# HGRN's diagonal level as a product of query and keys, summed by a square of ones in two fp32r passes, and products with the weights' low part last

## The chip, the core and the metric

The kernel runs on one core of one Trainium2 chip. The core has five engines that run side by side, each through its own list of instructions in order, and wait for each other on semaphores: TensorE (PE in the profile; its weight loads are listed apart as PEld), VectorE (DVE), ScalarE (ACT), GpSimd (POOL) and SyncE (SP), which issues the DMA transfers. Matrix products go into PSUM banks; everything else lies in SBUF. The metric is the device time of one execution in microseconds. Each version is run several times and the median is taken.

## The reference

Two transformer blocks on 256 tokens of width 1024, all in float32. The first has three parts side by side behind one large projection: HGRN2 (a gated linear recurrence in both directions), a spatial gating unit and two gates; then a feed-forward layer and a gated embedding. The second is a Fourier mixer, a feed-forward layer, a retention mixer and a feed-forward layer. What the change touches most is HGRN2's part inside a chunk, for each of 8 heads and each direction:

```python
b = jnp.cumsum(gc, axis=2)                       # gc: log of the forget gates
diff = b[:, :, :, None, :] - b[:, :, None, :, :]
decay = jnp.exp(jnp.minimum(diff, 0.0)) * mask[:, :, None]
scores = jnp.einsum('bhtk,bhsk,bhtsk->bhts', qc, kc, decay)
o_intra = jnp.einsum('bhts,bhsv->bhtv', scores, vc)
```

On the diagonal (t = s) the decay is one, so the score there is the plain sum over k of the query times the key, and for both directions together it is the query times the sum of the two keys. All other products are `x @ w` with float32 weights.

## The kernel before

**Numbers in two parts.** TensorE multiplies fp32r, a rounded form of float32, in one pass. So each operand is kept as a high and a low part (`w_hi`, `w_lo`; `ht`, `gt` and others have `_hi` and `_lo` too), and a product is three matmuls: low x by high w, high x by high w, high x by low w. The weights come as one stream of chunks of 1 MB through three raw buffers. For chunk w, ACT makes `w_hi` (`split_hi`, L1006), then DVE makes `w_lo` as raw less `w_hi` (`split_lo`, L1438), which also frees the raw buffer for the next transfer (SP, L398). Four chunks have a place in `w_hi` and `w_lo`. `tick(w)` on both engines makes the parts of chunk w + 4; on DVE a tick may also hold an `ada` step (L1447), a weight chunk of a small product done there. `wait_chunk` on TensorE waits for `w_lo`, and with it for `w_hi`.

**Order.** The order is written out by hand on each engine: what stands first runs first. TensorE's functions are `wide_chunk` (24 matmuls of 512 columns: two token tiles, four rows of weights, three parts), `feat` (the same turned, 48 matmuls of 256 columns), `outer` (a chunk for tile 0 or tile 1, 12 matmuls of 512 columns) and the small pieces between them. A result of 1024 columns lies in one of two PSUM pairs, which ACT or DVE has to evacuate before it is used again; small results lie in four banks `tp`, each claimed for a numbered job.

**HGRN in levels.** The heads are done in two halves of four. For a half, `head_gates` makes from three projections the query `qf`, `qb`, the keys `kf`, `kb` and the gates `tf`, `tb`. `levels` then builds the scores in eight levels: level 0 is the diagonal, level lv > 0 holds the pairs whose positions part in blocks of 2^(lv-1). On each level TensorE does a chunk of another projection (`zi`, `zg` in half 0, `ga`, `gb` in half 1) and then 8 float32 products of 128 x 128 of `sk` and `sq`, which the profile lists as 16 records (L697). ACT fills `sq` and `sk` for a level by four copies (`stage_level`, L1091 to L1094; one copy, L1084, for the queries of level 0) once TensorE has read the level before and DVE has updated queries and keys. DVE reads the scores into `at` through a mask (`take_scores`, L1659) and multiplies totals, queries and keys by the gates for the next level (L1648, L1628, L1638). In half 0, level 0, DVE also multiplies the gating unit's `u` (`gate_u`, L1769). ACT evacuates a pair on every odd level (L1015); in half 0, level 5, the function changes to Silu, for which ACT loads a table.

**The other places.** Behind HGRN `outer` multiplies by `wb` and `wa`; the tiles of `a_out` are turned on TensorE and split into `gt` in two halves for each token tile (L1024 on ACT, L1514 on DVE), and `wait_split("ta", 2)` waits for both. In the retention mixer's gate (`rg`, chunks 0 to 7) DVE multiplies head by head (`gated_head`, L2018), and TensorE turns the products from chunk 5 on; then `outer` multiplies by `ro`. `gate_rows` (L638) adds up a diagonal with a square of ones in two fp32r passes: two matmuls of 512 columns for each bank.

## Time and profile before

| | before |
|---|---|
| median of 3 runs | 1138.7 us (1138.3 to 1139.54) |
| profiled execution | 1139.04 us, span 1136.6 us |
| mean granted TensorE clock | 0.998 |
| TensorE busy | 1127.7 us, 99% |
| DVE busy | 852.0 us, 75% |
| ACT busy | 545.2 us, 48% |
| chain that ended last, TensorE's share | 94% |

The span runs from the first to the last instruction; the execution holds 2.4 us around it. Records of TensorE overlap, since their ends are modelled: how fast it goes is seen from start to start. A name like `w_lo<-raw,w_hi` says what is written and read.

### The profile page before, as it was taken

The numbers are of one execution on the slowest core, as the hardware profiler recorded it, in microseconds if no ns is written. First come the engines' busy times: TensorE is split into PE (matmuls) and PEld (weight loads), VectorE is DVE, ScalarE is ACT, GpSimd is POOL, SyncE is SP. The second block draws the span as 40 slices with busy tenths as digits, with TensorE's granted clock in tenths as the row PEclk, the third lists the DMA queues.
The fourth block names the chain that finished last, engine by engine and source line by source line (L and its number), as shares of the span: only waits on it lengthen the run. The fifth ranks groups of instructions, "written<-read, shape, count | busy, mean of one in ns | idle before, by whom it ended". The sixth has DMA issues, their size and how long they took to land.

```text
span 1136.6 us, 14091 instructions
## 1 busy us (share of the span) xinstructions
PE 1127.7 (99%) x5852; PEld 964.3 (85%) x5852; DVE 852.0 (75%) x958; ACT 545.2 (48%) x552; POOL 31.4 (3%) x51
## 2 busy tenths in 40 slices
PE   9999999999999999999999999999999999999997
PEld 8998998888888888889888888889988888888886
DVE  7899879977766768566677677479967866867685
ACT  6756456634744444355645353453332435444441
POOL 1000000000100000000000000000001000000000
PEclk9999999999999999999999999999999999999999
DMA  8864554448567777544477778558753754886760
GB/s 290 306 231 153 179 201 148 149 177 310 189 229 289 267 286 286 218 155 149 148 262 260 299 255 314 204 212 297 285 212 111 255 226 168 307 301 253 298 228 37
DMA packets 37966, 259.81 MB, mean 229 GB/s; under 512 B 4240, under 2 KB 4752, under 8 KB 7440
## 3 DMA queue, kind: packets, MB, share of 16 engines
q1 hardware_dynamic: 36000, 251.67, 60.1%
q0 software_dynamic: 1616, 7.08, 1.7%
q8 instruction: 46, 0.75, 0.3%
q10 hardware_dynamic: 288, 0.17, 0.1%
q14 instruction: 16, 0.13, 0.0%
HBM read 257.86 MB, written 1.05 MB: 228 GB/s over the span
## 4 chain that ended last, share of the span: by engine, by line
PE 94%; DVE 2%; DMA 2%; ACT 1%; issue 1%; POOLq 0%; POOL 0%; DVEq 0%; ACTq 0%
PE pair L477 47%; PE pair L542 20%; PE pair L503 10%; PE pair L558 4%; PE tp L606 3%; PE tp L697 3%; DMA raw<-stream 1%; PE tp L978 1%; ACT w_hi L1006 1%; PE pair L916 1%; PE tp L724 1%; DVE w_lo L1438 1%; PE tp L954 1%; PE tp L903 1%; PE pair L824 1%
## 5 line engine op out<-in xcount | busy, mean ns | idle before, releaser
L1438 DVE TENSOR_TENSOR w_lo<-raw,w_hi 128x2048 fp32r<-128x2048 f32 x180 | 409.0, 2288 | 77.5 <-ACT w_hi L1006 77.1
L1006 ACT ACTIVATE w_hi<-raw 128x2048 fp32r<-128x2048 f32 x180 | 344.3, 1917 | 228.4 <-DMA raw<-stream 140.6
L477 PE MATMUL pair<-w_hi,ht_lo 128*128 128x512 f32 x784 | 310.1, 396 | 0.0
L477 PE MATMUL pair<-w_lo,ht_hi 128*128 128x512 f32 x784 | 305.6, 390 | 0.0
L477 PE MATMUL pair<-w_hi,ht_hi 128*128 128x512 f32 x784 | 305.3, 389 | 0.0
L477 PEld LDWEIGHTS pair<-w_lo,ht_hi 128*128 128x128 f32 x784 | 147.1, 188 | 31.2
L477 PEld LDWEIGHTS pair<-w_hi,ht_lo 128*128 128x128 f32 x784 | 147.3, 188 | 29.4 <-DVE ht_lo L1498 0.5
L477 PEld LDWEIGHTS pair<-w_hi,ht_hi 128*128 128x128 f32 x784 | 147.4, 188 | 29.0
L1447 DVE SCALAR_TENSOR_TENSOR raw<-raw,crow 128x1024 f32<-128x1024 f32 x112 | 132.3, 1219 | 0.7 <-DMA raw<-stream 0.7
L542 PE MATMUL pair<-w_hi,gt_lo 128*128 128x512 f32 x272 | 107.1, 394 | 0.5 <-DVE w_lo L1438 0.3
L542 PE MATMUL pair<-w_lo,gt_hi 128*128 128x512 f32 x272 | 106.0, 390 | 0.0
L542 PE MATMUL pair<-w_hi,gt_hi 128*128 128x512 f32 x272 | 105.9, 389 | 0.0
L1124 ACT ACTIVATE prod<-pair 128x512 f32<-128x512 f32 x33 | 19.8, 599 | 153.6 <-PE pair L477 153.6
L1576 DVE TENSOR_TENSOR prod<-prod,pair 128x512 f32<-128x512 f32 x33 | 22.7, 688 | 93.9 <-ACT prod L1124 93.9
L503 PE MATMUL pair<-ht_hi,w_lo 128*128 128x256 f32 x304 | 86.4, 284 | 0.0
L503 PE MATMUL pair<-ht_lo,w_hi 128*128 128x256 f32 x304 | 86.0, 283 | 0.0
L503 PE MATMUL pair<-ht_hi,w_hi 128*128 128x256 f32 x304 | 86.0, 283 | 0.0
L542 PEld LDWEIGHTS pair<-w_hi,gt_lo 128*128 128x128 f32 x272 | 51.1, 188 | 11.7 <-DVE w_lo L1438 0.7
L542 PEld LDWEIGHTS pair<-w_lo,gt_hi 128*128 128x128 f32 x272 | 51.1, 188 | 10.7
L542 PEld LDWEIGHTS pair<-w_hi,gt_hi 128*128 128x128 f32 x272 | 51.1, 188 | 10.2
L503 PEld LDWEIGHTS pair<-ht_hi,w_hi 128*128 128x128 f32 x304 | 58.4, 192 | 0.0
L503 PEld LDWEIGHTS pair<-ht_hi,w_lo 128*128 128x128 f32 x304 | 58.3, 192 | 0.0
(289 smaller groups left out, 1370.2 us busy)
## 6 DMA issues: line engine op xcount, KB each, us to landing
raw<-stream SPq DMA_DIRECT2D x236, 1024.0 KB, 4.9
raw<-stream SPq DMA_DIRECT2D x8, 256.0 KB, 6.2
xres<-x SPq DMA_DIRECT2D x2, 512.0 KB, 5.0
prow<-rows POOLq DMA_DIRECT2D x1, 1024.0 KB, 10.6
xres<-x POOLq DMA_DIRECT2D x2, 512.0 KB, 4.9
dt<-decay POOLq DMA_DIRECT2D x1, 1024.0 KB, 10.8
csr<-dft POOLq DMA_DIRECT2D x1, 768.0 KB, 6.0
sgw<-sg_wT POOLq DMA_DIRECT2D x1, 512.0 KB, 5.8
```

What stands on the lines that cost most here:

```text
L477: mm = pe.matmul(pair[use % 2][:, t, :], a[:, 4 * c + k, t * P:(t + 1) * P], b[:, w % WS, k * 512:(k + 1) * 512], start=(c == 0 and k == 0 ...
L503: mm = pe.matmul(pair[use % 2][:, c, m * S:(m + 1) * S], a[:, k, m * P:(m + 1) * P], b[:, k, :], start=(k == 0 and n == 0), stop=(k == KT ...
L542: mm = pe.matmul(pair[(use + t) % 2][:, half, :], src(a, k0 + 2 * c + k, t), wsp[b][:, (w + c) % WS, k * D + half * 512:k * D + half * 512 ...
L558: mm = pe.matmul(dst, src(a, 2 * c + k, t), wsp[b][:, (w + c) % WS, k * D + a0:k * D + b0], start=(c == first and k == 0 and m == 0), stop ...
L606: mm = pe.transpose(tp[k % BANKS][:, n * P:(n + 1) * P], a, idn[:, 0:P])
L697: mm = pe.matmul(tp[k % BANKS][:, hd * P:(hd + 1) * P], sk[:, hd, s * P:(s + 1) * P], sq[:, hd, s * P:(s + 1) * P], start=True, stop=True)
L724: mm = pe.matmul(tp[k % BANKS][:, hd * P:(hd + 1) * P], at[:, s, hd, t * P:(t + 1) * P], vv[:, s, (HH * half + hd) * P:(HH * half + hd + 1 ...
L1006: sc.activation(w_hi[:, w % WS, :], raw[:, n % RAW, :], ACT.Copy).then_inc(hi_done, 1)
L1124: sc.activation(prod[:, j % 2, :, :], pair[(use + j) % 2][:, :, 0:256], ACT.Silu).then_inc(silu_done, 1)
L1438: v.tensor_tensor(w_lo[:, w % WS, :], raw[:, n % RAW, :], whi32[:, w % WS, :], ALU.subtract).then_inc(raw_done, 1)
L1447: ins = v.scalar_tensor_tensor(out=src, in0=src, scalar=1.0, in1=crow[:], op0=ALU.mult, op1=ALU.mult, accum_out=mod[:, 2 * a + half:2 * a ...
L1576: v.tensor_tensor(prod[:, j % 2, :, :], prod[:, j % 2, :, :], pair[(use + j) % 2][:, :, 256:512], ALU.mult).then_inc(evac[(use + j) % 2], 1)
```

## The change

**Diagonal level.** DVE now multiplies `sk = kf + kb` by `qf`, ACT rounds the product to `qk_hi`, DVE takes the rest as `qk_lo`, and TensorE sums both over the partitions with a square of ones: every row of the result holds the sums, and the mask takes the diagonal. This stands on TensorE behind the chunk of level 1 and right ahead of level 1's scores. The copy of `qf` to `sq` is gone; the copy to `qk_hi` stands on ACT behind the evacuation of the third projection and ahead of a `w_hi` split. DVE reads level 0's scores together with level 1's. `gate_u` moves from level 0 to level 4, and ACT waits for it (`b_out`) on level 5.

**Low part last.** For the first token tile of a chunk (`wide_first`, the first half of `feat`, `outer` at t = 0), TensorE waits for `w_hi` alone, does all products with it, then waits for `w_lo` and does those with `w_lo`. The numbers of matmuls stay.

**Two orders.** `wa` starts with one half of the split and waits for the other at chunk 2. `gated_head(0)` stands ahead of the tick of `rg` chunk 4 instead of behind its loop.

```diff
+            def wide_first(w, use, c):
+
+                pe.wait_ge(hi_done, pieces_done(w))
+                for n, (a, b) in enumerate(passes(ht, wsp)):
+                    if n == 2:
+                        wait_chunk(w)
+                    for k in range(4):
+                        pe.matmul(pair[use % 2][:, 0, :], a[:, 4 * c + k, 0:P], b[:, w % WS, k * 512:(k + 1) * 512],
+                                  start=(c == 0 and n == 0 and k == 0), stop=(c == 1 and n == 2 and k == 3))
...
             def wide_chunk(w, use, c):
-                wait_chunk(w)
                 if c == 0:
                     claim_pair(use)
-                for t in range(TT):
-                    wide_part(w, use, c, t)
+                wide_first(w, use, c)
+                wide_part(w, use, c, 1)
...
+                    if t == 0 and (c, t) not in middle:
+                        pe.wait_ge(hi_done, pieces_done(w + c))
+                        for n, (a, b) in enumerate([(1, 0), (0, 0), (0, 1)]):
+                            if n == 2:
+                                wait_chunk(w + c)
...
+                def own():
+                    pe.wait_ge(hg_qk, half + 1)
+                    for s in range(2):
+                        claim(job + s)
+                        for n in range(2):
+                            mm = pe.matmul(tp[(job + s) % BANKS][:], ones_r[:], qk[n][:, :, s * P:(s + 1) * P],
+                                           start=(n == 0), stop=(n == 1))
+                        mm.then_inc(tp_done, 1)
+
                 for lv in range(8):
                     wide_chunk(W0[name] + lv, USE[name] + lv // 2, lv % 2)
+                    if lv == 0:
+                        continue
+                    if lv == 1:
+                        own()
                     pe.wait_ge(hg_staged, 8 * half + lv + 1)
-                    if lv == 0:
-                        pe.wait_ge(hg_sk0, half + 1)
...
-                  before={(0, 0): lambda: wait_split("ta", 2), (0, 1): lambda: wait_split("ta", 4)},
+                  before={(0, 0): lambda: wait_split("ta", 1), (2, 0): lambda: wait_split("ta", 2),
+                          (0, 1): lambda: wait_split("ta", 4)},
...
                 if lv == 0:
-                    if half:
-                        act.wait_ge(tp_done, JOB["pa"] + 16)
-                    act.wait_ge(evac[USE["qa" if half == 0 else "qb"] % 2], USE["qa" if half == 0 else "qb"] // 2 + 1)
-                    sc.activation(sq[:], qf[:], ACT.Copy).then_inc(hg_staged, 1)
+                    act.wait_ge(hg_sk0, half + 1)
+                    sc.activation(qk[0][:], sk[:], ACT.Copy).then_inc(hg_staged, 1)
                     return
...
+                        if half == 0 and lv == 5:
+                            act.wait_ge(b_out, 2)
                         evacuate(dst, use, func)
...
-                v.tensor_tensor(sk[:], kf[:], kb[:], ALU.add).then_inc(hg_sk0, 1)
+                link(v.tensor_tensor(sk[:], kf[:], kb[:], ALU.add))
+                v.tensor_tensor(sk[:], sk[:], qf[:], ALU.mult).then_inc(hg_sk0, 1)
                 gates(1, tb)
                 dve.wait_ge(hg_staged, 8 * half + 1)
+                v.tensor_tensor(qk[1][:], sk[:], as_f32(qk[0][:]), ALU.subtract).then_inc(hg_qk, 1)
                 link(v.tensor_tensor(qb[:], qf[:], tb[:], ALU.mult))
                 v.tensor_tensor(qf[:], qf[:], tf[:], ALU.mult).then_inc(hg_qupd, 1)
...
                 for lv in range(8):
-                    take_scores(half, lv)
+                    if lv == 1:
+                        take_scores(half, 0)
+                    if lv:
+                        take_scores(half, lv)
...
-                    if half == 0 and lv == 0:
+                    if half == 0 and lv == 4:
                         gate_u()
                     tick(W0[name] + lv)
...
             for c in range(5):
+                if c == RH:
+                    gated_head(0)
                 tick(W0["rg"] + c)
...
-            gated_head(0)
             gated_head(1)
```

How this moves the instructions, at three places. First DVE in half 0, from the keys to the first updates, before (a bracket names the semaphores waited for: `step` is DVE's own last result, `hg_staged` ACT's copies):

```order
L1612 TENSOR_TENSOR sk<-kf,kb 128x1024 [waits step]
L1598 TENSOR_SCALAR tb<-tb,lbt 128x256 x4
L1601 TENSOR_SCALAR tb<-tb 128x1024 [waits step]
L1615 TENSOR_TENSOR qb<-qf,tb 128x1024 [waits hg_staged,step]
L1616 TENSOR_TENSOR qf<-qf,tf 128x1024 [waits step]
L1438 TENSOR_TENSOR w_lo<-raw,w_hi 128x2048 [waits hi_done]
L1659 COPY_PREDICATED at<-msk,tp 128x4x128 [waits tp_done] x2
L1628 TENSOR_TENSOR qf<-qf,tf 128x512 [waits hg_staged,hg_qupd]
```

and now, where lines of the kernel have shifted:

```order
L1663 TENSOR_TENSOR sk<-kf,kb 128x1024 [waits step]
L1664 TENSOR_TENSOR sk<-sk,qf 128x1024 [waits step]
L1649 TENSOR_SCALAR tb<-tb,lbt 128x256 x4
L1652 TENSOR_SCALAR tb<-tb 128x1024 [waits step]
L1667 TENSOR_TENSOR qk_lo<-sk,qk_hi 128x1024 [waits hg_staged,step]
L1668 TENSOR_TENSOR qb<-qf,tb 128x1024
L1669 TENSOR_TENSOR qf<-qf,tf 128x1024 [waits step]
L1489 TENSOR_TENSOR w_lo<-raw,w_hi 128x2048 [waits hi_done]
L1681 TENSOR_TENSOR qf<-qf,tf 128x512 [waits hg_staged,hg_qupd]
```

A product and a subtraction have come in ahead of qb and qf, and the reading of level 0's scores has gone from here.

ACT in half 0 around level 5, before:

```order
L1094 ACTIVATE sk<-kb 128x32x16
L1015 ACT_TABLE_LOAD
L1015 ACTIVATE zg<-pair 128x2x512 [waits w_used]
L1006 ACTIVATE w_hi<-raw 128x2048 [waits w_used,landed0]
L1091 ACTIVATE sq<-qf 128x16x32 [waits tp_done,hg_kupd,hg_qupd]
```

and now:

```order
L1143 ACTIVATE sk<-kb 128x32x16
L1061 ACT_TABLE_LOAD [waits b_out]
L1061 ACTIVATE zg<-pair 128x2x512 [waits w_used]
L1052 ACTIVATE w_hi<-raw 128x2048 [waits w_used,landed0]
L1140 ACTIVATE sq<-qf 128x16x32 [waits tp_done,hg_kupd,hg_qupd]
```

The wait for `gate_u` stands ahead of the table load; both stand ahead of level 6's copies.

TensorE in half 0 between the chunk of level 1 and that of level 2, before:

```order
L477 MATMUL pair<-w_lo,ht_hi 128x512
L697 MATMUL tp<-sq,sk 128x128 [waits sgu_read,hg_staged]
L697 MATMUL tp<-sq,sk 128x128 x3
L697 MATMUL tp<-sq,sk 128x128 [waits sgu_read]
L697 MATMUL tp<-sq,sk 128x128 x3
L477 MATMUL pair<-w_hi,ht_lo 128x512 [waits evac0,raw_done]
```

and now:

```order
L727 MATMUL tp<-qk_hi,ones 128x512 [waits lo_done,hg_qk]
L727 MATMUL tp<-qk_lo,ones 128x512
L727 MATMUL tp<-qk_hi,ones 128x512 [waits rows_read]
L727 MATMUL tp<-qk_lo,ones 128x512
L742 MATMUL tp<-sq,sk 128x128 [waits sgu_read,hg_staged]
L742 MATMUL tp<-sq,sk 128x128 x3
L742 MATMUL tp<-sq,sk 128x128 [waits sgu_read]
L742 MATMUL tp<-sq,sk 128x128 x3
L482 MATMUL pair<-w_hi,ht_lo 128x512 [waits hi_done,evac0]
```

The sums of level 0 have come in ahead of level 1's scores; behind the chunk of level 0 nothing stands any more, and the chunk of level 2 begins with a wait for w_hi.

## Rows read from the trace of the kernel before

**Rows 1.** The page's first part, whole span: busy time, share, instructions of each engine.
```profile
PE 1127.7 (99%) x5852; PEld 964.3 (85%) x5852; DVE 852.0 (75%) x958; ACT 545.2 (48%) x552; POOL 31.4 (3%) x51
```

**Rows 2.** The chain that ended last; columns: start us, length us, what.
```profile
83.56 1.78 PE tp L697 x16
...
836.66 0.92 PE tp L638 x4
```

**Rows 3.** Timeline of TensorE; columns: start, length, instruction, in brackets idle time before.
```profile
83.40 0.27 PE L697 MATMUL tp<-sq,sk 128*128 128x128 f32 x1
...
119.60 0.27 PE L697 MATMUL tp<-sq,sk 128*128 128x128 f32 x1
...
182.11 0.27 PE L697 MATMUL tp<-sq,sk 128*128 128x128 f32 x1
...
244.94 0.50 PE L542 MATMUL pair<-w_hi,gt_lo 128*128 128x512 f32 x1 [0.25 <-DVE gt_lo L1514]
...
881.27 0.33 PE L606 MATMUL tp<-idn,gg 128*128 128x128 f32 x1 [0.16 <-DVE gg L2018]
...
925.52 0.39 PE L542 MATMUL pair<-w_lo,gt_hi 128*128 128x512 f32 x1
926.20 0.50 PE L542 MATMUL pair<-w_hi,gt_lo 128*128 128x512 f32 x1 [0.29 <-DVE w_lo L1438]
```

**Rows 4.** Timeline of VectorE (DVE), around the levels and the three waits.
```profile
77.33 1.23 DVE L1615 TENSOR_TENSOR qb<-qf,tb 128x1024 f32<-128x1024 f32 x1
78.59 1.23 DVE L1616 TENSOR_TENSOR qf<-qf,tf 128x1024 f32<-128x1024 f32 x1
79.73 2.29 DVE L1438 TENSOR_TENSOR w_lo<-raw,w_hi 128x2048 fp32r<-128x2048 f32 x1
81.94 1.34 DVE L1659 COPY_PREDICATED at<-msk,tp 128x512 f32<-128x512 uint8 x2
83.17 0.68 DVE L1628 TENSOR_TENSOR qf<-qf,tf 128x512 f32<-128x512 f32 x1
...
85.57 1.28 DVE L1769 TENSOR_TENSOR u<-u,vg 128x512 f32<-128x512 f32 x2
86.77 2.28 DVE L1438 TENSOR_TENSOR w_lo<-raw,w_hi 128x2048 fp32r<-128x2048 f32 x1
...
114.29 2.28 DVE L1438 TENSOR_TENSOR w_lo<-raw,w_hi 128x2048 fp32r<-128x2048 f32 x1
...
136.59 2.29 DVE L1438 TENSOR_TENSOR w_lo<-raw,w_hi 128x2048 fp32r<-128x2048 f32 x1 [3.97 <-ACT w_hi L1006]
...
234.79 1.22 DVE L1812 TENSOR_TENSOR gb<-gb,pair 128x1024 f32<-128x1024 f32 x1 [1.60 <-PE pair L542]
...
243.59 1.29 DVE L1514 TENSOR_TENSOR gt_lo<-tp,gt_hi 128x512 fp32r<-128x512 f32 x2 [2.09 <-ACT gt_hi L1024]
...
877.72 2.29 DVE L1438 TENSOR_TENSOR w_lo<-raw,w_hi 128x2048 fp32r<-128x2048 f32 x1 [1.52 <-ACT w_hi L1006]
```

**Rows 5.** Timeline of ScalarE (ACT), in the levels.
```profile
72.72 1.92 ACT L1006 ACTIVATE w_hi<-raw 128x2048 fp32r<-128x2048 f32 x1
...
81.57 0.66 ACT L1094 ACTIVATE sk<-kb 128x512 f32<-128x512 f32 x1
...
110.25 1.28 ACT L1015 ACT_TABLE_LOAD   x1
112.56 1.03 ACT L1015 ACTIVATE zg<-pair 128x1024 f32<-128x1024 f32 x1 [1.03 <-PE pair L477]
...
116.85 0.62 ACT L1094 ACTIVATE sk<-kb 128x512 f32<-128x512 f32 x1
...
180.25 0.66 ACT L1094 ACTIVATE sk<-kb 128x512 f32<-128x512 f32 x1
```

**Rows 6.** Busy time by stretch: us, PE, PEld, DVE, ACT, POOL, clock (PEclk), DMA, GB/s.
```profile
1130.20:1132.30 2.10, 0.00 (x0) 0.00 (x0) 1.44 (x4) 0.51 (x2) 0.35 (x1) 1.00 0.00 0
1132.40:1136.60 4.20, 0.00 (x0) 0.00 (x0) 1.54 (x3) 0.00 (x0) 0.10 (x1) 0.50 0.34 125
```

More of the change, by code:

```diff
@@ L499, in feat @@
                 wv = [a[:, w % WS, :].rearrange("p (k n) -> p k n", k=KT) for a in wsp]
-                for m in range(2):
+                for n, (a, b) in enumerate([(wv[0], ht[1]), (wv[0], ht[0]), (wv[1], ht[0])]):
+                    if n == 2:
+                        wait_chunk(w)
                     for k in range(KT):
-                        for n, (a, b) in enumerate(passes(wv, ht)):
-                            mm = pe.matmul(pair[use % 2][:, c, m * S:(m + 1) * S], a[:, k, m * P:(m + 1) * P],
-                                           b[:, k, :], start=(k == 0 and n == 0), stop=(k == KT - 1 and n == 2))
+                        pe.matmul(pair[use % 2][:, c, 0:S], a[:, k, 0:P], b[:, k, :], start=(k == 0 and n == 0),
+                                  stop=(k == KT - 1 and n == 2))
+                for k in range(KT):
+                    for n, (a, b) in enumerate(passes(wv, ht)):
+                        mm = pe.matmul(pair[use % 2][:, c, S:2 * S], a[:, k, P:2 * P], b[:, k, :],
+                                       start=(k == 0 and n == 0), stop=(k == KT - 1 and n == 2))
                 mm.then_inc(w_used, 1)
@@ L528, in outer, with whole_part @@
                 m = max(0, n - 4)
+                last = n - 1
                 order = [(c, t) for c in range(m) for t in range(TT)] + [(c, t) for t in range(TT) for c in range(m, n)]
-                for c, t in order:
-                    if (c, t) in before:
-                        before[c, t]()
-                    if t == 0:
-                        wait_chunk(w + c)
-                    if c == 0:
-                        claim_pair(use + t)
+                def whole_part(c, t):
                     for half in range(2):
```

38 lines of the change are left out of this document (31 added, 7 removed).

## The prediction

> **What bounds the kernel now.** I read the share of busy time first [rows 1]: TensorE (PE) is busy 99% of the span, VectorE (DVE) 75%, ScalarE (ACT) 48%. So a microsecond of matmuls saved is a microsecond of kernel, if nothing else comes late in its place. Next the chain that ended last [rows 2]: in the eight levels of one half of HGRN it is TensorE alone, a chunk of 24 matmuls of 512 columns and then 16 records of 128 columns, 1.78 us. Then the timeline of TensorE [rows 3]: a matmul's record is 0.39 long (925.52), though the next one starts 0.23 after it where nothing waits (4 in 0.92 [rows 2]). The bracketed idle time counts from the record's end, so a wait costs 0.16 more than it says, and the first record behind it is longer too (0.50). Behind the start-up only three waits for another engine are long enough to be listed: at 244.94, at 881.27 and at 926.20. Last, the timelines of DVE and ACT in the levels [rows 4, 5]: DVE stands there without a gap, and ACT's copies into sq and sk, which the scores of a level wait for, end little ahead of TensorE.
>
> **What TensorE is spared.** The diagonal level was 16 records, 1.78 us. It is now 4 matmuls of 512 columns, for which the nearest row is the gate's rows, also a square of ones against fp32r: 4 in 0.92 [rows 2]. Saved: 0.86 us a half, 1.72 in all, if the rest of the level keeps up. The reordered products are as many as before, of the same shapes, so I take them at nothing. A wait whose semaphore is already up costs nothing that shows: the scores at 83.40 [rows 3] stand behind two and have no idle time ahead.
>
> **The three waits that go.** At 244.94 TensorE waits for the second half of a split (gt_lo); it now needs the first of DVE's two operations alone, which take 1.29 together from 243.59 [rows 4] and so ended 0.6 us earlier: saved 0.25 + 0.16 + 0.11 (longer record) = 0.52. At 881.27 it waits for gg; the product now stands ahead of the split at 877.72 instead of behind it, in the 1.52 us in which DVE waited for ACT there [rows 4]; two of gg's four operations, about 1.25 us, fit in: 0.16 + 0.16 + 0.05 = 0.37. At 926.20 it waits for w_lo, ready at 926.15; the low part is now wanted 8 matmuls (1.8 us) later than the first: 0.29 + 0.16 + 0.11 = 0.56. Together 1.45 us. Everywhere else low-part-last removes a wait that wasn't there.
>
> **What is added: the first level in half 0.** Before, sq was a copy made long ahead, and the level's sk needed one addition. Now DVE has to make (kf+kb)*qf and its low part, both ahead of qb and qf. An operation of this size takes 1.26 where the next waits for it (77.33 to 78.59) and 1.14 where not (78.59 to 79.73) [rows 4]. The addition of sk turns from the second kind into the first, the product adds 1.14, the subtraction 1.14: 0.12 + 1.14 + 1.14 = 2.40 us. ACT's copy to qk_hi (about 1.0) runs under DVE's gates and hides. But qf ends 2.40 later, and level 1's copies start on it: the last ended at 81.57 + 0.66 = 82.23 [rows 5], and will end at 84.63. TensorE wanted them at 83.40 [rows 3] and will want them 0.86 earlier, at 82.54. It starts at 84.68 instead of 83.40, plus 0.05 for the cold start: **1.33 us later than before**, a stall of 2.2 where 0.86 was to be won.
>
> **The second place in half 0: gate_u.** DVE is saturated, so its delay lasts. Its updates for level 1 wait for the copies (84.63, seen at 84.72) instead of starting at 83.17, and end 2.40 later at 87.12. A split (2.21, from 79.73 to 81.94) and the displaced reading of the diagonal's scores (1.23, 81.94 to 83.17) bring it to 90.56 where it was at 86.77 + 2.21 = 88.98: 1.58 late (gate_u's 1.20 at 85.57 has gone from there). It keeps that to the end of level 5's key updates, 114.29 + 1.58 = 115.87. There gate_u now stands, to 117.15. ACT, which evacuated a pair at 112.56, has a new wait for gate_u (b_out) ahead of that. The built order shows the wait ahead of the **table load** too, which before ran in the open at 110.25 and now takes its 1.28 behind the wait: evacuation at 118.46. Behind it on ACT are a split and the copies of level 6: from 112.56 to 116.85 + 0.62 that was 4.91 us [rows 5], so they end at 123.37. TensorE, 1.33 late, would ask at 119.60 + 1.33 = 120.93 and starts at 123.42: 3.82 + 0.05 = **3.87 us later than before** (this holds the 1.33). What is late next is DVE: it is then about as late as TensorE, plus 1 to 2 us; its idle 3.97 us ahead of 136.59 [rows 4] takes that up, and no TensorE step waits on it before.
>
> **Half 1.** The same head without gate_u: copies ended at 180.25 + 0.66 = 180.91, now 183.31; TensorE starts at 183.36 instead of 182.11: **1.25 + 0.05 = 1.30 us later**. DVE's wait for the copies and the displaced reading make it 1.55 + 1.23 = 2.8 us late against TensorE's 1.30. In both halves the copies of the other levels lie further ahead of TensorE than level 1's 1.17 us, and I reckon that they bear the 1.5 between the two. DVE's 1.60 idle at 234.79 takes the rest up, so the wait at 244.94 isn't reached by it.
>
> **Moves that I cost at nothing.** The w_hi split that now stands behind the qk_hi copy comes 5 us later (72.72 [rows 5] to 77.6). Its w_lo is made when DVE gets there, now at 82.13, and TensorE wants the chunk two chunks behind level 1's scores: that is the cover, some 7 us. The stream's transfers follow DVE's splits, so they shift by the same 1.5 to 2.4 us; a chunk is loaded four chunks ahead. No DMA, no Pool instruction and nothing on SP is moved.
>
> **Sum.** Against the profiled execution (1139.04 us, span 1136.6): + 3.87 + 1.30 - 1.45 = **+3.7 us**, 1142.8. The runs shown have their median at 1138.7, 0.3 below it, so I forecast **1142.4**. Its own range is 1141.3 to 1143.4: the extra behind a stall is 0 to 0.11 at three places, the diagonal's four matmuls change nothing while a stall follows them, and DVE's additions may be 10% off over 2.4 and 1.6.
>
> **Rivals.** (a) The added DVE work is hidden: then 1138.7 - 1.72 - 1.45 = **1135.5**. It decides at the slack of level 1's copies, 83.40 - 82.23 = 1.17 less the 0.86 that TensorE comes earlier: 0.3 us, against 2.40 added. Against it: three DVE operations would have to be 0.1 us long, and rows of just this size are 1.1 to 1.2. For it: only that the copies might begin without qf, which the order of ACT denies. Chance 0.09.
> (b) Only the stalls at level 1 come; gate_u is early enough, or the table load hides. Then half 0 keeps 1.33: 1138.7 + 1.33 + 1.30 - 1.45 = **1139.9**. It needs DVE to make up over 2 us between 90 and 116, where its timeline has no gap. Chance 0.08.
> (c) The clock falls in a stall. TensorE did nothing from 1130.2 to 1132.3 and was granted 1.00 of 2.4 GHz; from 1132.4 on it was granted 0.50, 1.2 GHz [rows 6]. The stalls forecast here are 2.2, 2.5 and 2.2 us long, about where that fall stands. While the clock is down the same matmuls take about twice as long; a fall for some 4 us costs 2. One in the first stall would be swallowed by the second; one in the second or third gives **1144.4**, both 1146.4. Against it: matmuls stand thick on either side, and at the end none followed. Chance 0.18. The Trainium skill ("TensorE: Matmul & The Clock Gate", section "HAM oscillation — how this bites in real kernels") has it that idle gaps between bursts of matmuls put the clock back to its low level, and that every return is paid for. By that rule the time would be (c)'s; the trace agrees that idleness brings the fall, and has no gap inside the kernel that would show how it treats one of 2 us.
> (d) A copy of a later level is late too, or a saving is not had (DVE is over 1 us later than TensorE in half 1, or when the head outputs are due): up to 1.5 more, **1143.9**. Chance 0.10.
> (e) Low-part-last doesn't shorten anything, since the waits at 244.94 and 926.20 only move inside the chunk: 1143.5, in (d)'s price. The rows speak against it: w_lo is up 1.4 us before it is wanted.
>
> **Chances.** Forecast 0.55, (a) 0.09, (b) 0.08, (c) 0.18, (d) with (e) 0.10. Two in ten are left out by 1139.0 to 1145.0: (a) below, half of (c) above. A change of 0.2% (2.3 us, about what a measurement of this kernel can tell from none) parts 1136.4 and 1141.0: faster 0.09, (b) and a little of the forecast's own spread within it 0.15, slower 0.76.
>
> **What would show it.** In the profile after: TensorE idle some 2 us ahead of level 1's scores in both halves and 2.3 to 2.5 ahead of level 6's in half 0, put down to ACT's copies into sk; DVE's qf ending near 82.2; the table load near 117 instead of 110; no listed waits for gt_lo, gg and w_lo; the four ones matmuls in 0.92. Wrong it would be if TensorE reached level 1's scores later than its copies, if the table load stood at 110 or if 0.50 stood in the clock's row in the middle of the span.

## The result, and the profile of the changed kernel

The changed kernel takes **1143.4 us** in the median of 6 runs (1142.0 to 1145.4), the kernel before 1137.9 in 6 runs beside them: a ratio of 1.0047, 95% interval 1.0037 to 1.0057. It is slower by 5.5 us, half a per cent. Forecast were 1142.4, and 1139.0 to 1145.0. In a second set of runs it was 1142.8 (5 runs) against 1137.6, again 1.0047.

The profiled execution took 1141.98 us, span 1139.5. The page's first part, which answers [rows 1], shows that TensorE did less and that the kernel is longer all the same:

```profile
PE 1126.6 (99%) x5828; PEld 961.7 (84%) x5828; DVE 856.4 (75%) x962; ACT 544.6 (48%) x552; POOL 31.4 (3%) x51
```

The waits of TensorE (what waited, for whom: us in all, times, the longest). The three of before at 244.94, 881.27 and 926.20 [rows 3] are gone, and three new ones stand there, all for ScalarE's last copy into sk:

```profile
PE tp L742 <- ACT sk L1143: 4.6, 3, 1.9
PE tp L778 <- POOL expo L411: 1.0, 1, 1.0
PE tp L640 <- DMA idn<-ident: 0.7, 1, 0.7
```

The timeline of TensorE at these three places: the first and the last sum of ones (L727), then level 1's scores (L742); the last matmul ahead of level 6's scores and these; level 1 again in half 1. It answers [rows 3]:

```profile
80.64 0.39 PE L727 MATMUL tp<-qk_hi,ones 128*128 128x512 f32 x1
...
81.34 0.39 PE L727 MATMUL tp<-qk_lo,ones 128*128 128x512 f32 x1
83.67 3.61 PE L742 MATMUL tp<-sq,sk 128*128 128x128 f32 x16 [1.94 <-ACT sk L1143]
...
121.38 0.39 PE L489 MATMUL pair<-w_lo,ht_hi 128*128 128x512 f32 x1
122.51 2.05 PE L742 MATMUL tp<-sq,sk 128*128 128x128 f32 x16 [0.74 <-ACT sk L1143]
...
184.05 0.39 PE L727 MATMUL tp<-qk_lo,ones 128*128 128x512 f32 x1
186.37 2.05 PE L742 MATMUL tp<-sq,sk 128*128 128x128 f32 x16 [1.94 <-ACT sk L1143]
```

Two things are to be seen. The stalls stand where they were forecast, though the middle one is short. And the 16 records at 83.67 took 3.61 us where the same 16 take 2.05 at 186.37: the clock fell. The windows view (us, then busy time of PE, PEld, DVE, ACT, POOL, then the granted clock) of that stretch has it at half, 1.2 GHz, where the rest of the levels has 1.00:

```profile
83.80:87.10 3.30, 3.30 (x17) 3.30 (x18) 3.30 (x5) 2.52 (x2) 0.00 (x0) 0.51 0.78 263
```

VectorE's timeline, which answers [rows 4]. The product (L1664) and the subtraction (L1667) stand ahead of qf (L1669), and gate_u (L1822) now behind level 5's key updates:

```profile
74.34 1.22 DVE L1664 TENSOR_TENSOR sk<-sk,qf 128x1024 f32<-128x1024 f32 x1
...
77.62 1.23 DVE L1667 TENSOR_TENSOR qk_lo<-sk,qk_hi 128x1024 fp32r<-128x1024 f32 x1
...
80.01 1.23 DVE L1669 TENSOR_TENSOR qf<-qf,tf 128x1024 f32<-128x1024 f32 x1
...
114.90 1.28 DVE L1822 TENSOR_TENSOR u<-u,vg 128x512 f32<-128x512 f32 x2
```

ScalarE's timeline, which answers [rows 5]. The table load ran at 110.25 before, right behind the copies; it now waits 4.88 us for gate_u and has the evacuation, a split and level 6's copies behind it:

```profile
70.85 1.02 ACT L1266 ACTIVATE kb<-pair 128x1024 f32<-128x1024 f32 x1
...
82.96 0.66 ACT L1143 ACTIVATE sk<-kb 128x512 f32<-128x512 f32 x1
...
110.77 0.62 ACT L1143 ACTIVATE sk<-kb 128x512 f32<-128x512 f32 x1
116.27 1.28 ACT L1061 ACT_TABLE_LOAD   x1 [4.88 <-DVE u L1822]
117.56 1.03 ACT L1061 ACTIVATE zg<-pair 128x1024 f32<-128x1024 f32 x1
...
121.84 0.62 ACT L1143 ACTIVATE sk<-kb 128x512 f32<-128x512 f32 x1
```

**Executions start differently.** This evacuation of kb, ahead of all that the diagonal's change touches, began at 70.85; in the execution on which the sum was made, ScalarE's timeline has it at 71.82:

```profile
71.82 1.02 ACT L1218 ACTIVATE kb<-pair 128x1024 f32<-128x1024 f32 x1
```

The kernel before was therefore profiled once more (`before_again`, below): there kb began at 70.84 and the execution took 1137.82. Against this twin with the same start the changed kernel's span is 1139.5 - 1135.5 = 4.0 us longer; against the first profile, put on the same start, 1139.5 - (1136.6 - 0.97) = 3.9. The sum was 3.7.

### The profile page after: what moved, and what is told of

Read it like the earlier page. It is cut to its first block, busy times and chain, and to the rows that moved or that the text cites. A ratio compares the mean times of both kernels' runs of the same rounds, so it can differ in the third digit from the quotient of the medians.

```text
span 1139.5 us, 14049 instructions
## 1 busy us (share of the span) xinstructions
PE 1126.6 (99%) x5828; PEld 961.7 (84%) x5828; DVE 856.4 (75%) x962; ACT 544.6 (48%) x552; POOL 31.4 (3%) x51
## 4 chain that ended last, share of the span: by engine, by line
PE 93%; DVE 3%; issue 2%; ACT 1%; DMA 0%; DVEq 0%; POOLq 0%; POOL 0%; ACTq 0%
PE pair L489 26%; PE pair L482 18%; PE pair L572 11%; PE pair L554 11%; PE pair L519 5%; PE pair L515 5%; PE pair L592 4%; PE tp L640 3%; PE tp L742 1%; PE tp L1024 1%; PE pair L962 1%; PE tp L769 1%; PE tp L1000 1%; PE tp L949 1%; PE pair L869 1%
## 5 line engine op out<-in xcount | busy, mean ns | idle before, releaser
L489 PE MATMUL pair<-w_hi,ht_lo 128*128 128x512 f32 x456 | 177.9, 390 | 0.0
L489 PE MATMUL pair<-w_lo,ht_hi 128*128 128x512 f32 x456 | 177.6, 389 | 0.0
L489 PE MATMUL pair<-w_hi,ht_hi 128*128 128x512 f32 x456 | 177.4, 389 | 0.0
L489 PEld LDWEIGHTS pair<-w_hi,ht_lo 128*128 128x128 f32 x456 | 85.6, 188 | 17.9 <-DVE ht_lo L1549 0.5
L482 PE MATMUL pair<-w_hi,ht_lo 128*128 128x512 f32 x328 | 92.6, 404 | 0.0
L482 PE MATMUL pair<-w_hi,ht_hi 128*128 128x512 f32 x328 | 88.0, 390 | 0.0
L482 PE MATMUL pair<-w_lo,ht_hi 128*128 128x512 f32 x328 | 87.8, 390 | 0.0
L482 PEld LDWEIGHTS pair<-w_hi,ht_lo 128*128 128x128 f32 x328 | 58.6, 189 | 9.8
L554 PE MATMUL pair<-w_hi,gt_lo 128*128 128x512 f32 x136 | 53.3, 392 | 0.0
L554 PE MATMUL pair<-w_lo,gt_hi 128*128 128x512 f32 x136 | 53.0, 390 | 0.0
L554 PE MATMUL pair<-w_hi,gt_hi 128*128 128x512 f32 x136 | 52.9, 389 | 0.0
L417 POOL TENSOR_TENSOR st<-st,expo 128x1 f32<-128x1 f32 (+1 forms) x32 | 23.7, 743 | 913.7 <-DVE st L1516 572.3
L519 PE MATMUL pair<-ht_hi,w_lo 128*128 128x256 f32 x152 | 43.0, 283 | 0.0
```

The lines of the kernel that those rows point to most:

```text
L417: g.tensor_tensor(st[:, r, 2, 0:w], st[:, r, 1, 0:w], expo[:, 0:w], ALU.pow).then_inc(rstd_done, 1)
L482: pe.matmul(pair[use % 2][:, 0, :], a[:, 4 * c + k, 0:P], b[:, w % WS, k * 512:(k + 1) * 512], start=(c == 0 and n == 0 and k == 0), stop= ...
L489: mm = pe.matmul(pair[use % 2][:, t, :], a[:, 4 * c + k, t * P:(t + 1) * P], b[:, w % WS, k * 512:(k + 1) * 512], start=(c == 0 and k == 0 ...
L519: mm = pe.matmul(pair[use % 2][:, c, S:2 * S], a[:, k, P:2 * P], b[:, k, :], start=(k == 0 and n == 0), stop=(k == KT - 1 and n == 2))
L554: mm = pe.matmul(pair[(use + t) % 2][:, half, :], src(a, k0 + 2 * c + k, t), wsp[b][:, (w + c) % WS, k * D + half * 512:k * D + half * 512 ...
```

## The experiments

Theory: nearly all of the loss is three stalls of TensorE ahead of level 1 (twice) and level 6, made by VectorE's two added operations ahead of qf and by gate_u with the table load; the rest is the clock that falls in stalls. Rivals: the reordered products cost time themselves; the sums of ones do; the spread has nothing to do with the clock.

### Half of the change at a time

`e1_no_diag` is the kernel before with only this kind of edit, in wide_chunk, feat and outer, with the wait for ta's split cut in two and gated_head(0) moved:

```diff
-                wait_chunk(w)
+                pe.wait_ge(hi_done, pieces_done(w))
...
+                for n, (a, b) in enumerate(passes(ht, wsp)):
+                    if n == 2:
+                        wait_chunk(w)
```

> The kernel before with only the reordered products (the weights' low part last, the split wait in wa cut in two, gated_head(0) moved up); the diagonal level stays as it was. The stall theory: the products do the same matmuls in another order and cost nothing, the three waits of before at 244.94 (0.52), 881.27 (0.37) and 926.20 (0.56) are gone, so 1137.9 - 1.45 = 1136.4 us, and no new wait on TensorE. The rival, that the new order itself costs time (other weights loaded one after the other, the low part's matmuls late), wants 1138.5 us or more here, since some of the +5.5 us must then lie in these products.

Measured: 1136.9 us (11 runs), ratio 0.9995, interval 0.9986 to 1.0003. Waits of TensorE:

```profile
PE tp L765 <- POOL expo L409: 1.0, 1, 1.0
PE tp L638 <- DMA idn<-ident: 0.5, 1, 0.5
```

Nothing new, and none of the three left. By the medians the gain is 0.6 us, below what can be told from no change; by the traces it is 1.3 to 1.4: from the start of level 1's scores to the last matmul 1127.39 - 82.34 = 1045.05 us, against 1128.78 - 82.43 = 1046.35 in before_again and 1129.86 - 83.40 = 1046.46 in the first profile. The reordered products cost nothing; the first rival falls.

`e2_diag_only` is the kernel before with all the other edits:

```diff
+                link(v.tensor_tensor(sk[:], kf[:], kb[:], ALU.add))
+                v.tensor_tensor(sk[:], sk[:], qf[:], ALU.mult).then_inc(hg_sk0, 1)
...
+                v.tensor_tensor(qk[1][:], sk[:], as_f32(qk[0][:]), ALU.subtract).then_inc(hg_qk, 1)
...
-                    if half == 0 and lv == 0:
+                    if half == 0 and lv == 4:
                         gate_u()
```

> The kernel before with only the diagonal level changed (product, two passes of ones, gate_u at level 4, ScalarE's wait for b_out). The stall theory: the measured +5.5 us and the 1.45 us of the waits that are not won back here, 1137.9 + 5.5 + 1.4 = 1144.8 us, with three TensorE waits of about 1.9, 0.7 to 2.5 and 1.9 us ahead of the scores of levels 1, 6 and 1. Without any loss to the clock it would be 1137.9 + 5.2 = 1143.1 us. The rival (the reordered products cost) wants 1142.5 us or less.

Measured: 1144.0 us (5 runs), before 1137.5, ratio 1.0057 (1.0044 to 1.0070). Its waits have the three stalls and, besides, those for gt_lo and gg, as before:

```profile
PE tp L710 <- ACT sk L1110: 4.6, 3, 2.0
...
PE pair L544 <- DVE gt_lo L1532: 0.2, 1, 0.2
PE tp L608 <- DVE gg L2041: 0.2, 1, 0.2
```

That is 0.8 us less than expected, and more than 1142.5, where the rival would have it. The loss is the diagonal's, and the other half of the change gives back about a microsecond of it. The wait for w_lo that before had at 926.20 is not in this list, though the products stand here in their old order: w_lo was made by 929.20, and the matmul that needs it started at 931.34.

### gate_u back at its place

`e3_gate_early`, against the changed kernel:

```diff
-                    if half == 0 and lv == 4:
+                    if half == 0 and lv == 0:
                         gate_u()
...
-                        if half == 0 and lv == 5:
-                            act.wait_ge(b_out, 2)
```

> The changed kernel with gate_u back at level 0 and ScalarE's wait for b_out gone; everything else as changed. By the prediction's terms the stall ahead of level 6 goes and those of level 1 stay: 1137.9 - 3.2 + 1.33 + 1.30 + 2.5 of it that come back only if DVE's 2.56 us now delay another level; if none is delayed, 1139.9 us, plus what the clock takes in the first stall, about 1.7 us as in the profiled execution, which nothing swallows any more: 1141.6 us. If instead gate_u at level 0 falls due right behind the already late level 1, level 2 is late by up to 2.5 us and the time stays near 1143. ScalarE's wait of 4.9 us ahead of the table load should be gone and the sigmoid-to-Silu table load start at once behind the copies of level 5.

Measured: 1140.4 us (7 runs, 1139.3 to 1142.6), before 1137.5, ratio 1.0027 (1.0016 to 1.0038), where the changed kernel has 1.0047: 2.3 us less. The wait ahead of level 6 is gone: 3.9 us in two waits are left. The table load runs right behind level 5's copies:

```profile
111.51 0.62 ACT L1143 ACTIVATE sk<-kb 128x512 f32<-128x512 f32 x1
112.15 1.28 ACT L1061 ACT_TABLE_LOAD   x1
114.63 1.02 ACT L1061 ACTIVATE zg<-pair 128x1024 f32<-128x1024 f32 x1 [1.20 <-PE pair L489]
```

The profiled execution took 1142.59, though, and here the clock fell in both stalls, also behind the second (this row of the windows view is of half 1):

```profile
186.30:189.50 3.20, 3.20 (x15) 2.91 (x14) 3.20 (x4) 2.81 (x3) 0.00 (x0) 0.51 0.77 307
```

Of the 7 runs the two longest, 1142.6 and 1142.4, have a mean clock of 0.996 and the other five, 1139.3 to 1141.0, of 0.998 or 0.999. The four runs at 0.999 took 1139.3 to 1140.4, around the 1139.9 that was expected without a fall; the two longest lie above the 1141.6 expected with one fall, and the profiled one of them had two. The other branch, level 2 late, is not seen.

### The table load alone

`e5_table_early`, against the changed kernel (`tiny` is a new tile of four numbers that nothing reads):

```diff
                         if half == 0 and lv == 5:
+                            sc.activation(tiny[:], col[:, 0:4], ACT.Silu)
                             act.wait_ge(b_out, 2)
```

> The changed kernel with one Silu of four numbers put ahead of ScalarE's wait for b_out, so that the table load of 1.28 us stands ahead of that wait instead of behind it. The theory: level 6's copies end 1.28 us earlier. In executions in which TensorE was not held up before, the stall ahead of level 6 falls from 2.5 to 1.2 us; in those like the profiled one, with 0.9 us left of it, it goes. So 0.9 to 1.3 us less than the changed kernel of the same call. If instead VectorE's gate_u alone made level 6 late and the table load was beside it, the time stays that of the changed kernel.

Measured: 1141.2 us (5 runs) against 1142.8 for the changed kernel beside it: 1.6 less, where 0.9 to 1.3 was expected. ScalarE's and then TensorE's timeline:

```profile
112.99 1.28 ACT L1293 ACT_TABLE_LOAD   x1
116.15 0.21 ACT L1293 ACTIVATE tiny<-col 128x4 f32<-128x4 f32 x1 [1.87 <-PE pair L490]
117.80 1.03 ACT L1062 ACTIVATE zg<-pair 128x1024 f32<-128x1024 f32 x1 [1.44 <-DVE u L1824]
...
122.08 0.62 ACT L1144 ACTIVATE sk<-kb 128x512 f32<-128x512 f32 x1
```

```profile
123.19 1.95 PE L743 MATMUL tp<-sq,sk 128*128 128x128 f32 x16
```

The load is hidden and the 16 records at 123.19 have no idle time ahead; in this execution TensorE had lost time to a fall in the first stall, as in the changed kernel's. The wait for gate_u is still there, 1.44 us. The intervals of the two ratios overlap (1.0022 to 1.0047 here, 1.0034 to 1.0060 there), so the size rests on the trace: from the start of kb (72.43 here) to the end of level 6's copies it is 122.08 + 0.62 - 72.43 = 50.27 us, in the changed kernel 121.84 + 0.62 - 70.85 = 51.61, 1.34 more. The table load is a good half of the second stall, gate_u's place the rest.

### Clock and stalls apart

`e6_keep_warm`, against the changed kernel. The added matmuls write a PSUM bank that the scores then overwrite:

```diff
+                    warm_up = 9 if lv == 1 else 10 if lv == 6 and half == 0 else 0
+                    if warm_up:
+                        claim(job + 2 * lv)
+                    for _ in range(warm_up):
+                        pe.matmul(tp[(job + 2 * lv) % BANKS][:], ones_r[:], qk[0][:, :, 0:P], start=True, stop=True)
                     pe.wait_ge(hg_staged, 8 * half + lv + 1)
```

> The changed kernel with matmuls of 512 columns that nothing reads (0.23 us each) in TensorE's stalls: nine ahead of the wait for level 1's copies in each half, ten ahead of that for level 6's in the first. They fill the stalls and do not lengthen them by themselves. If the clock falls because TensorE stands still there, no record at half clock is left but the last one at the end, no execution is above 1142, and the median is before + 3.7 = 1141.2 to 1141.6 us on this chip, against 1143 for the changed kernel. If the falls have nothing to do with the stalls, falls and the spread to 1145 remain. If the whole +5.5 is stall and the clock has no part, the time stays 1143.

Measured: 1142.3 us (5 runs, 1142.1 to 1142.9), before 1137.6, ratio 1.0040 (1.0027 to 1.0053). TensorE in half 0 and half 1, and the same windows row as above:

```profile
82.01 2.26 PE L741 MATMUL tp<-qk_hi,ones 128*128 128x512 f32 x9
84.15 2.05 PE L747 MATMUL tp<-sq,sk 128*128 128x128 f32 x16
...
120.49 2.49 PE L741 MATMUL tp<-qk_hi,ones 128*128 128x512 f32 x10
122.95 2.05 PE L747 MATMUL tp<-sq,sk 128*128 128x128 f32 x16
...
184.71 2.26 PE L741 MATMUL tp<-qk_hi,ones 128*128 128x512 f32 x9
186.84 2.05 PE L747 MATMUL tp<-sq,sk 128*128 128x128 f32 x16
```

```profile
83.80:87.10 3.30, 3.30 (x24) 2.81 (x23) 2.99 (x6) 3.30 (x4) 0.00 (x0) 1.00 0.64 209
```

The clock stays at 1.00, the spread is 0.8 us instead of 3.2, and all five runs have a mean clock of 0.999. The stalls are now bare, and the middle one has its whole length: 122.95 - 120.49 = 2.46 us. The median is 0.7 to 1.1 above what was expected from before + 3.7. A part is this program's start (kb at 71.29, 0.45 later than in before_again).

`after_more` is the changed kernel again, timed beside e5 and e6.

> The changed kernel again, beside the others of this call. If the clock falls in one stall in some executions and in two or three in others, each fall some 1.5 us, the times stand in steps between 1141 (none, or one that the next stall swallows) and 1146 us and the mean clock is lower in the longer ones: 0.999 or 0.998 below 1142.5, 0.996 or 0.997 above. If the spread has another cause, time and clock are unrelated.

Measured: 1142.2, 1142.4 and 1142.8 us with a mean clock of 0.999, 1143.4 with 0.997, 1145.4 with 0.996. In the first set of runs: 1142.4 at 0.999; 1142.0 and 1143.4 at 0.997; 1143.4, 1143.8 and 1145.4 at 0.996. So a lower clock goes with a longer time in the main, with one clear exception, the profiled 1142.0, whose fall in the first stall was swallowed by the second. The profile of after_more (1143.43) has one fall too, in the same place, the same three waits of 4.6 us, and a start 1.46 us later (kb at 72.31): 1141.98 + 1.46 = 1143.44. That gives the size of the start.

The mean clock also tells roughly how many falls a run had. The eight profiles without a fall inside have 0.998 or 0.999, the three with one 0.997 or 0.998, the two with two 0.996. By this estimate the four of the changed kernel's 11 runs at 0.999 had no fall at all, and took 1142.2 to 1142.8; the four at 0.996 had more than one.

`e9_warm_gate` is e3_gate_early with the nine matmuls at level 1 alone:

```diff
+                    warm_up = 9 if lv == 1 else 0
```

> e3_gate_early (gate_u back at level 0) with the nine unread matmuls in each of its two stalls. If the clock's falls make e3's spread of 1139.3 to 1142.6, no record at half clock is left between start and end, the spread shrinks under 1 us, and the span from the start of level 1's scores in half 0 to the last matmul is 1048.0 - 1.6 - 1.6 = 1046.5 us against 1049.7 in e3's profiled execution and 1046.5 in before's. Median: e6's 1142.34 less the stall of level 6, 2.5: 1139.8. If the falls come from elsewhere, it stays at 1140.4 with the spread.

Measured: 1140.2 us (11 runs, 1139.4 to 1141.2), before 1138.3, ratio 1.0018 (1.0009 to 1.0028). The median was missed by 0.4 us and the spread of 1.7 is not under 1, while before itself, beside it, spread over 2.1 (1137.3 to 1139.4). But no run has a clock below 0.998, and the trace has no half clock. From level 1's scores to the last matmul it takes 1132.01 - 85.22 = 1046.8 us, e3 with its two falls 1133.43 - 83.75 = 1049.7. Nearly all of the difference is the two falls: **one costs 2.9 / 2 = 1.45 us.**

### The work ahead of qf

`e10_sub_behind`, against e3_gate_early. ScalarE's wait for hg_qk moves from ahead of level 1's copies to between the query's and the keys':

```diff
-                v.tensor_tensor(qk[1][:], sk[:], as_f32(qk[0][:]), ALU.subtract).then_inc(hg_qk, 1)
                 link(v.tensor_tensor(qb[:], qf[:], tb[:], ALU.mult))
                 v.tensor_tensor(qf[:], qf[:], tf[:], ALU.mult).then_inc(hg_qupd, 1)
+                v.tensor_tensor(qk[1][:], sk[:], as_f32(qk[0][:]), ALU.subtract).then_inc(hg_qk, 1)
```

> e3_gate_early with the subtraction (1.14 us) moved behind qf's product, and ScalarE's wait for it moved between the query's copies and the keys'. The term of the prediction: VectorE's work ahead of qf is what delays level 1, microsecond for microsecond, until another input is late. Level 1's first copy then waits for w_hi's split (ends 1.0 us before qf did) and not for qf: the scores start 0.9 us earlier in each half than e3's, the wait of 2.1 us shrinks to about 0.6 ahead of the sums of ones and 0.5 ahead of the scores: 1140.4 - 1.8 = 1138.6 us, or 1138.0 if the shorter waits bring no fall of the clock. If the delay of level 1 came from the ones matmuls or from ScalarE's copy instead, nothing is won: 1140.4.

Measured: 1138.7 us (11 runs), before 1138.3, ratio 1.0004 (0.9995 to 1.0013), as expected. TensorE's timeline:

```profile
81.49 0.39 PE L489 MATMUL pair<-w_lo,ht_hi 128*128 128x512 f32 x1
82.38 0.50 PE L727 MATMUL tp<-qk_hi,ones 128*128 128x512 f32 x1 [0.50 <-DVE qk_lo L1667]
...
83.66 2.05 PE L742 MATMUL tp<-sq,sk 128*128 128x128 f32 x16
...
98.99 2.05 PE L742 MATMUL tp<-sq,sk 128*128 128x128 f32 x16 [0.36 <-ACT sk L1143]
```

The wait is 0.50 instead of 1.95, for the low part, and the half clock is gone with it. The 1.14 us of VectorE taken from the path to qf bring level 1's scores 1.12 us earlier: from the start of kb they are 83.66 - 71.93 = 11.73 us, in e9_warm_gate, which has no fall either, 85.22 - 72.37 = 12.85. But it is not a microsecond of kernel in each half. A new wait of 0.36 shows at 98.99, level 3: with TensorE earlier, VectorE's lateness comes up there. By the starts of level 7's scores (128.10 and 227.06 here, 128.95 and 229.03 in e9, each less its kb), half 0 keeps 0.4 of it and half 1 adds 1.1; together 1.5, as the medians have it (1138.7 against 1140.2). The prediction had counted this reserve of the later levels as enough.

### The diagonal at another place

`e4_diag_late`, against the changed kernel: the sum of the keys goes into a tile of its own, the query is copied to another by ScalarE as before, and product, split and sums of ones run late. gate_u is back at level 0 and ScalarE's wait for b_out is gone, as in e3, where that alone removed level 6's stall. On VectorE:

```diff
-                link(v.tensor_tensor(sk[:], kf[:], kb[:], ALU.add))
-                v.tensor_tensor(sk[:], sk[:], qf[:], ALU.mult).then_inc(hg_sk0, 1)
+                v.tensor_tensor(own_s[:], kf[:], kb[:], ALU.add).then_inc(hg_sk0, 1)
...
+                    if lv == 4:
+                        dve.wait_ge(hg_sk0, half + 1)
+                        v.tensor_tensor(own_s[:], own_s[:], own_q[:], ALU.mult).then_inc(hg_prod, 1)
+                    if lv == 5:
+                        dve.wait_ge(hg_qhi, half + 1)
+                        v.tensor_tensor(qk[1][:], own_s[:], as_f32(qk[0][:]), ALU.subtract).then_inc(hg_qk, 1)
```

> The changed kernel with the diagonal's product, split and sums of ones moved to where VectorE and ScalarE have time: keys' sum and a copy of the query are kept in two tiles at 88 and 92 KB, the product is taken after level 4's updates, its high part after level 6's copies, the low part at level 5's end, and the ones matmuls stand ahead of level 7's scores; gate_u stays at level 0. If the stalls in front of levels 1 and 6 are the whole cost, none is left and each half saves its 0.86 us: 1137.9 - 1.72 - 1.45 = 1134.7 us. If the sums of ones or the product cost time by themselves (ports, banks, the weights' loads), the time stays above 1137. If the extra DVE work of 2.3 us makes a later level late, a wait of up to 2 us shows ahead of level 6's or 7's scores: 1136 to 1139.

Measured: 1136.7 us (11 runs), before 1137.5, ratio 0.9993 (0.9984 to 1.0002). The expectation of 1134.7 was missed by 2. TensorE's timeline:

```profile
80.47 0.39 PE L498 MATMUL pair<-w_lo,ht_hi 128*128 128x512 f32 x1
81.36 2.05 PE L751 MATMUL tp<-sq,sk 128*128 128x128 f32 x16 [0.50 <-ACT sk L1153]
...
125.84 1.95 PE L751 MATMUL tp<-sq,sk 128*128 128x128 f32 x16
```

Levels 6 and 7 wait for nothing, so the late product is hidden. But level 0's 16 records had also been the cover of level 1's copies: without them TensorE comes 1.7 us earlier and the copies are ready 1.2 us ahead of its old time, as the rival (a) had it in numbers. Per half 1.70 go, 0.91 for the sums of ones come, and 0.66 of wait and 0.11 behind it come too: nothing is left. The sum of the expectation had no term for this.

`e8_late_level1`, against e4_diag_late: level 1's scores are called from within the next chunk.

```diff
                 for n, (a, b) in enumerate(passes(ht, wsp)):
+                    if n == 1 and between:
+                        between()
```

> The kernel e4_diag_late with the scores of level 1 moved behind the first four matmuls (0.9 us) of the next chunk of products, in both halves. In e4 TensorE waits 0.66 and 0.65 us ahead of level 1's scores, since level 0's 16 matmuls no longer stand there. If that is all that was missing to its forecast, both waits go and the time is 1.3 us below e4's: 1135.4 us on the same scale. If instead level 2's copies now come late because level 1's scores are 0.9 us later, a wait of up to 0.9 us shows ahead of level 2 and nothing is won.

Measured: **1135.4 us** (11 runs, 1134.8 to 1136.5), before 1137.6, ratio 0.9979 (0.9970 to 0.9988): faster than both kernels. TensorE's timeline:

```profile
81.44 1.07 PE L493 MATMUL pair<-w_hi,ht_lo 128*128 128x512 f32 x4
82.35 1.95 PE L750 MATMUL tp<-sq,sk 128*128 128x128 f32 x16
```

No wait behind the start-up is listed. From the start of kb to the last matmul it takes 1126.45 - 71.66 = 1054.79 us, in e1_no_diag, which has the same products and the old diagonal, 1127.39 - 70.76 = 1056.63. The diagonal as sums of ones is worth what the forecast gave it, 2 x 0.86 us (1.84 measured), once no engine waits for it.

### The kernel before, once more

`before_again` is the kernel before without an edit.

> The kernel before, profiled once more. The profiled execution on which the prediction's sum was made took 1139.04 us, its timed ones 1137.5 in the median. If the start (TensorE waiting for its first weights, at 1.2 GHz until 9.4 us there) is what differs, this execution has the level 1 scores of half 0 start up to 1.5 us earlier than 83.40, the same 46 us by 46 us behind it, and no record at half clock between the start and the end. If before has falls of the clock too, such records show.

Measured: 1138.7 us (11 runs) beside 1138.3 for before, ratio 1.0002 (0.9993 to 1.0011). The profiled one took 1137.82. ScalarE's timeline, then TensorE's waits:

```profile
70.84 1.02 ACT L1218 ACTIVATE kb<-pair 128x1024 f32<-128x1024 f32 x1
```

```profile
...
PE pair L542 <- DVE gt_lo L1514: 0.3, 1, 0.3
PE tp L606 <- DVE gg L2018: 0.2, 1, 0.2
```

The start was 1.0 us earlier, not the 1.5 that was allowed for. There is no half clock inside. The runs of this label fall into two groups, four from 1137.6 to 1137.8 and seven from 1138.7 to 1139.1.

The wait for w_lo that stood at 926.20 is not in this list, but TensorE's timeline has it, shorter:

```profile
924.60 0.39 PE L542 MATMUL pair<-w_lo,gt_hi 128*128 128x512 f32 x1
925.08 0.50 PE L542 MATMUL pair<-w_hi,gt_lo 128*128 128x512 f32 x1
```

The second matmul starts 0.48 us behind the first where 0.23 is the rule, and the next one 0.34 behind it: 0.25 + 0.11 = 0.36 us. The idle time behind the first one's record, 0.09, was too short to be listed.

What makes a start early or late can be read from the same eight matmuls in the start-up, first here, then in the first profile of before:

```profile
6.62 1.06 PE L791 MATMUL tp<-ones 128*128 128x128 f32 x8
```

```profile
7.21 1.92 PE L791 MATMUL tp<-ones 128*128 128x128 f32 x8
```

In the late start they ran at about half the pace (the next matmul came 1.70 us behind the first of them instead of 0.89): TensorE came to its full clock later. The changed kernel's two profiles differ in the same way, 1.06 at 6.49 in the early one and 1.91 at 7.42 in after_more.

## Why the prediction was right, step by step

**The levels.** Times of after with 0.97 us added for its earlier start, against the forecast:

| step | forecast | measured |
|---|---|---|
| level 1's copies end, half 0 | 84.63 | 82.96 + 0.66 + 0.97 = 84.59 |
| scores of level 1 start | 84.68 | 83.67 + 0.97 = 84.64 |
| key updates of level 5 end | 115.87 | 114.90 + 0.97 = 115.87 |
| evacuation to zg starts | 118.46 | 117.56 + 0.97 = 118.53 |
| level 6's copies end | 123.37 | 121.84 + 0.62 + 0.97 = 123.43 |
| scores of level 6 start | 123.42 | 122.51 + 0.97 = 123.48 |

Half 1 adds 186.37 - 122.51 = 63.86 where before had 182.11 - 119.60 = 62.51 [rows 3]: 1.35, forecast 1.30. So each term of the levels stands within 0.1 us. What the forecast left at "0 to 0.11" behind a stall is 0.11 wherever no fall hides it: 2.05 for 16 records against 1.95.

**The sums of ones** take 0.23 each, 0.92 for the four, as the row of the gate's rows had it. **The reordered products** cost nothing (e1).

**The three waits.** By the traces e1 gains 1.3 to 1.4 us, of 1.45 forecast. Two waits went as forecast. The third is a property of the kernel, but its size is not: it cost 0.56 us in the first profile and 0.36 in before_again. And that the products' new order removed it is not shown. In e2, with the old order, it is gone as well, and in e1 w_lo was ready at 923.16, 0.7 us before the chunk's first matmul at 923.88, so that either order would have done.

**Rival (c), the clock,** came true in part, and its sign, about 0.50 in the clock's row in the middle of the span, had been named as one of being wrong. In five profiles of kernels with the unfilled first stall (after, after_more, e2, e3, e5) the clock fell in the first stall every time. In the third it fell in e3 and e5, and not in after, after_more and e2. It fell in none of the middle ones, 0.74 us. As the prediction said, a fall in the first is swallowed by the second: level 6's scores stood at 122.51 and would have stood there without it (e6: 122.95 - 0.44 for the start = 122.51). Priced at 2 us, a fall costs 1.45. Not every run has such a fall (by the mean clock about a third of the changed kernel's have none), but the chance of 0.18 was too low; what saved the forecast is that the commonest fall is swallowed.

**Where the medians' remaining 1.2 to 1.6 us lie.** The forecast's 1142.4 is 1.0 us below the measured 1143.4, and even that is partly luck: its base of 1138.7 was a median of three runs, where the six have 1137.9. From base to result it forecast + 3.7 and the medians have + 5.5 and + 5.2; the high base hid 0.8 of that. The traces of like start differ by 3.9 to 4.0. The traces show two causes: falls in the third stall, 1.45 each (seen in e3 and e5; the changed kernel's runs at 1145.4 are by their mean clock of this kind, but neither was profiled), and the start. before had a late start in one profile of two, 1.0 us later, the changed kernel in one of two, 1.46 us later. The step that failed is therefore the last one: "The runs shown have their median at 1138.7, 0.3 below it". That sum stands on one execution of one program, and leaves out that starts differ and that falls inside come on top. A late start is one in which TensorE comes to its full clock later (before_again, above). With e6, whose clock never falls inside, still 4.7 us separate the medians where its levels give 3.8. Whether the changed kernel starts late more often, and why, is open: the runs without a profile don't show their start, and no experiment was made on it.

**Rivals (a), (b), (d), (e).** (a) fell: its slack was 0.3 us and e4 measured it from the other side. (b) is e3: 1139.9 was named and 1140.4 measured, with falls in some runs. (d) did not come in the changed kernel, but e10 shows where the reserve ends: level 3. (e) is refuted for gt_lo by e1, which gains 0.5 us there, and open for w_lo, as said above.

## What to carry to other kernels

When a cheaper form of a step needs more work from the engine that feeds the next step, compare the added work with the slack of what it stands ahead of; here 2.4 us stood against 0.3, in the very spot where the saved 0.86 us had been the cover. The same arithmetic gained its 0.8 us a half once the product ran where its result was wanted late and four other matmuls took the place of the cover. And a term below a microsecond that stands in one profiled execution should be looked up in a second one before it goes into a sum, in the starts of the matmuls and not only in the list of waits: a wait of 0.36 us was too short for the list.

## What the runs showed of the hardware

- A stall of 2.1 to 2.3 us between dense matmuls can bring TensorE's clock from 2.4 to 1.2 GHz for some 3.3 us (83.80 to 87.10); the first such stall did in 5 profiles of 5, the last in 2 of 5, though by their mean clock some of the runs without a profile had no fall. Matmuls that nothing reads, put into the stall, prevented it (e6, e9), and waits of 0.4 to 0.7 us brought none (e4, e10, the middle one of the changed kernel). The Trainium skill ("TensorE: Matmul & The Clock Gate", "HAM oscillation — how this bites in real kernels") says that idle gaps between bursts put the clock back and each return is paid for. The gaps of its own example are longer than these; these traces agree, with 1.45 us for one fall, and show that a stall of 2.1 us can be enough.
- TensorE can come to its full clock earlier or later at the start of the same code: eight matmuls of the start-up took 1.06 us at 6.62 in before_again and 1.92 us at 7.21 in before, and kb followed at 70.84 and at 71.82, 1.0 us later. Between the two profiles of the changed kernel it is 1.46 us.
- The fall's price is not paid in idle time: in the changed kernel the records that run at half speed begin with the scores themselves at 83.67 (3.61 us against 2.05), and they and the next chunk pay.
- A table load that precedes an activation behind two waits ran behind the first of them when that was VectorE's gate_u (4.88 us), and ran at once when that wait was gone (e3, 112.15, with 1.20 us of waiting left behind it). A tiny activation of the same function ahead of the wait moved it (e5). The Trainium skill ("ScalarE: Activation LUTs", "What ACT_TABLE_LOAD costs") gives about 1.28 us for the load, as in the rows, and a further 1.38 us of drain; here zg started 0.01 us behind the load's end (116.27 + 1.28, 117.56), and in e3 the load started 0.02 us behind the copy ahead of it (111.51 + 0.62, 112.15), so no such drain shows on either side.
